# Eight weight parts queued at once in idle memory, at the head of a two-block transformer kernel

## The reference

```python
c_act = silu(c)                                   # [1, 1024]
for i in range(2):
    mod = c_act @ ada_w[i] + ada_b[i]             # ada_w[i]: 1024 x 6144
    sh_a, sc_a, g_a, sh_f, sc_f, g_f = split(mod, 6)
    h = rms_norm(x, norm_g[i, 0]) * (1 + sc_a) + sh_a
    y = attention_i(h, qkv weights, output weights, rel_bias)
    x = x + g_a * rms_norm(y, norm_g[i, 1])
    h = rms_norm(x, norm_g[i, 2]) * (1 + sc_f) + sh_f
    x = x + g_f * rms_norm(swiglu(h), norm_g[i, 3])
# then the third block, whose weights stream in the same way
```

## Time and profile before

| what | value |
|---|---|
| median of 3 runs | 1074.29 us (1073.21 to 1080.11) |
| span of the profiled execution | 1076.4 us |
| PE busy | 994.9 us (92%) |
| DVE busy | 690.4 us (64%) |
| ACT busy | 507.4 us (47%) |
| DMA, mean rate over the span | 193 GB/s |
| DMA, mean rate in the first 80 us | 337 GB/s |

### The profile page before, as it was taken

How to read it: one execution, slowest core, us unless ns; L and a number is a source line. 1 busy time by engine, 2 the same in 40 slices (tenths; PEclk the granted TensorE clock), 3 DMA queues, 4 the chain that set the end, 5 groups by cost and what they waited for, 6 DMA issues and landing times.

```text
span 1076.4 us, 18734 instructions
## 1 busy us (share of the span) xinstructions
PE 994.9 (92%) x7732; PEld 956.7 (89%) x7732; DVE 690.4 (64%) x724; ACT 507.4 (47%) x609; POOL 51.3 (5%) x103
## 2 busy tenths in 40 slices
PE   1799997999999997999889999999899999999996
PEld 1699995999999986999869999999799899999996
DVE  4787865778668747688755444444697654554554
ACT  2455435444344355566654343344565544444464
POOL 3010001001000001000010000000100000000000
PEclk9999989999999998999989999999999999999998
DMA  9997862598779741754215554556135465556511
GB/s 334 354 317 273 313 217 91 196 312 276 257 272 325 256 139 57 237 183 149 91 67 169 183 195 163 188 193 205 61 132 182 124 190 193 164 188 194 171 65 40
DMA packets 128186, 207.67 MB, mean 193 GB/s; under 512 B 4498, under 2 KB 101907, under 8 KB 128147
## 3 DMA queue, kind: packets, MB, share of 16 engines
q1 hardware_dynamic: 116818, 163.59, 45.9%
q0 software_dynamic: 11328, 43.53, 11.7%
HBM read 206.04 MB, written 1.06 MB: 192 GB/s over the span
## 4 chain that ended last, share of the span: by engine, by line
PE 83%; DVE 6%; ACT 4%; issue 3%; DMA 3%; POOL 1%; SPq 0%; DVEq 0%; POOLq 0%; ACTq 0%
PE ps L501 25%; PE ps L502 25%; PE ps L503 25%; PE ps L563 4%; DMA raw<-in_moba_w_qkv 2%; DVE rstd L1208 1%; ACT w_hi L857 1%; DMA ada_raw<-in_ada_w 1%; PE ps L678 1%; PE ps L576 1%; PE ps L652 1%; POOL xt L474 1%; DVE ada_sum L1177 1%; DVE w_lo L1164 1%; DVE y L1227 1%
## 5 line engine op out<-in xcount | busy, mean ns | idle before, releaser
L1164 DVE TENSOR_TENSOR w_lo<-raw,w_hi 128x2048 fp32r<-128x2048 f32 x145 | 332.0, 2291 | 220.2 <-ACT w_hi L857 220.0
L501 PE MATMUL ps<-h_hi,w_hi 128*128 128x256 f32 x1376 | 397.3, 289 | 23.0 <-DVE h_lo L1222 12.8
L857 ACT ACTIVATE w_hi<-raw 128x2048 fp32r<-128x2048 f32 x145 | 276.7, 1910 | 267.4 <-PE ps L503 265.9
L502 PE MATMUL ps<-h_lo,w_hi 128*128 128x256 f32 x1376 | 392.7, 285 | 0.0
L503 PE MATMUL ps<-h_hi,w_lo 128*128 128x256 f32 x1376 | 392.4, 285 | 0.0
L501 PEld LDWEIGHTS ps<-h_hi,w_hi 128*128 128x128 f32 x1376 | 267.6, 194 | 27.4 <-issue 23.3
L502 PEld LDWEIGHTS ps<-h_lo,w_hi 128*128 128x128 f32 x1376 | 267.9, 195 | 0.3
L503 PEld LDWEIGHTS ps<-h_hi,w_lo 128*128 128x128 f32 x1376 | 267.5, 194 | 0.0
L501 PE MATMUL ps<-o_hi,w_hi 128*128 128x256 f32 x528 | 155.1, 294 | 5.5 <-DVE o_lo L1482 2.3
L502 PE MATMUL ps<-o_lo,w_hi 128*128 128x256 f32 x528 | 150.0, 284 | 0.0
L503 PE MATMUL ps<-o_hi,w_lo 128*128 128x256 f32 x528 | 149.9, 284 | 0.0
(11 more groups left out here) (227 smaller groups left out, 1063.2 us busy)
## 6 DMA issues: line engine op xcount, KB each, us to landing
raw<-in_ffn_w_in SPq DMA_DIRECT2D x44, 1024.0 KB, 5.2
ada_raw<-in_ada_w POOLq DMA_DIRECT2D x40, 1024.0 KB, 5.8
raw<-in_ffn_w_out SPq DMA_DIRECT2D x22, 1024.0 KB, 5.0
raw<-in_w_up SPq DMA_DIRECT2D x16, 1024.0 KB, 5.5
raw<-in_w_down SPq DMA_DIRECT2D x16, 1024.0 KB, 4.9
raw<-in_moba_w_qkv SPq DMA_DIRECT2D x12, 1024.0 KB, 7.3
raw<-in_diff_w_qkv SPq DMA_DIRECT2D x12, 1024.0 KB, 5.5
raw<-in_w_in SPq DMA_DIRECT2D x6, 1024.0 KB, 5.4
```

The costliest lines, as they stand in the source:

```text
L501: T.matmul(out_ap, hi_s, hi_m, start=start, stop=False, skip_group_check=True)
L502: T.matmul(out_ap, hi_s, lo_m, start=False, stop=False, skip_group_check=True)
L857: A.activation(w_hi[:, n.place], raw[:, n.place], ACT.Copy).then_inc(slab_hi, 1)
L1164: V.tensor_tensor(w_lo[:, n.place], raw[:, n.place], w_hi[:, n.place].bitcast(F32), ALU.subtract).then_inc(slab_lo, 1)
```

## The change

Each of the first eight parts has a place that nothing else uses at that time: part 0 the tile `bias`, part 1 one half in `qkv` and one in `prob`, parts 2, 3 and 4 the places 2, 1 and 0 of `raw`, parts 5, 6 and 7 the places 0, 1 and 2 of `ada_raw`. SP issues all eight with no wait between them, `x` still behind part 1. Because a place may now be in two tiles, each part is issued as two transfers of 512 KB in place of one of 1 MB. The fourteen small vectors are issued behind part 7; before, they stood between part 5 and part 6. Slab 0 waits for `ada_acc` 10, slab 1 for 8, slab 2 for 6. The two loads of `bias` wait for `ada_acc` 2. The computation is the same.

```diff
         def first_mod_place(m):
-            if 3 <= m < 6:
-                return raw[:, m - 3].rearrange("p (k n) -> p k n", k=2), first_mods[m % 6]
-            return ada_raw[:, (m + 1) % ADA_RING], first_mods[m % 6]
+            if m == 0:
+                return bias_flat[:, 0:D], bias_flat[:, D:2 * D]
+            if m == 1:
+                return flat_qkv[:, 0:D], flat_prob[:, 0:D]
+            if m < 5:
+                return raw[:, 4 - m, 0:D], raw[:, 4 - m, D:2 * D]
+            place = (m + 1) % ADA_RING
+            return ada_raw[:, place, 0], ada_raw[:, place, 1]
...
                 else:
-                    sp.wait_ge(ada_acc, 2 * (n.first + 4))
+                    sp.wait_ge(ada_acc, 2 * (5 - n.first))
...
             def first_mod(m):
-                buffer, done = first_mod_place(m)
-                if m >= 6:
-                    sp.wait_ge(ada_acc, 2 * (m - 5))
-                sp.dma_start(buffer, rows(ada_w[0][:, ds(m // 4 * D, D)], m % 4)).then_inc(done, 16)
+                part = rows(ada_w[0][:, ds(m // 4 * D, D)], m % 4)
+                for k, buffer in enumerate(first_mod_place(m)):
+                    sp.dma_start(buffer, part[:, k]).then_inc(first_mods[m], 16)

             first_mod(0)
             first_mod(1)
             sp.dma_start(x_tok, ...).then_inc(x_loaded, 16)
-            for m in range(2, 6):
+            for m in range(2, 8):
                 first_mod(m)
...
             for dst, r, n, src in vectors:
                 sp.dma_start(dst[r:r + n, :], src).then_inc(rows_loaded, 16)
-            first_mod(6)
-            first_mod(7)
...
             for first, at, width in ((0, 0, S), (P, S, P)):
+                pool.wait_ge(ada_acc, 2)
                 src = bass.AP(line_dram.tensor, first, [[1, P], [LINE, HEADS], [1, width]])
                 pool.dma_start(bias[:, :, at:at + width], src).then_inc(bias_loaded, 16)
```

More of the change, by code:

```diff
@@ L226, in build @@
         bias_flat = bias[:].rearrange("p a b -> p (a b)")
+        flat_qkv = qkv[:].rearrange("p a b c -> p (a b c)")
+        flat_prob = prob[:].rearrange("p a b -> p (a b)")
         lru_h = bias_flat[:, 0:CT * S].rearrange("p (t s) -> p t s", t=CT)
@@ L247, in build @@
         slab_hi, slab_lo, slab_done = sem("slab_hi"), sem("slab_lo"), sem("slab_done")
-        first_mods = [sem(f"first_mods_{i}") for i in range(6)]
+        first_mods = [sem(f"first_mods_{i}") for i in range(8)]
         ada_loaded = [sem(f"ada_loaded_{i}") for i in range(ADA_RING)]
@@ L1165, in split_lo, with ada @@
                                 ALU.subtract).then_inc(slab_lo, 1)
-            def ada(m, place, count, slot, scalars, fresh, buffer=None, loaded=None):
-                buffer = ada_raw[:, place] if buffer is None else buffer
-                dve.wait_ge(loaded or ada_loaded[place], count)
+            def ada(m, place, count, slot, scalars, fresh, first_halves=None):
+                halves = first_halves or (ada_raw[:, place, 0], ada_raw[:, place, 1])
+                if first_halves:
+                    dve.wait_ge(first_mods[m], 32)
+                else:
+                    dve.wait_ge(ada_loaded[place], count)
                 for k in range(2):
                     if fresh and k == 0:
-                        V.tensor_scalar(ada_sum[:, slot], buffer[:, k], scalars[k], None, ALU.mult)\
+                        V.tensor_scalar(ada_sum[:, slot], halves[k], scalars[k], None, ALU.mult)\
                             .then_inc(ada_acc, 1)
@@ L1176, in ada @@
                         dve.wait_ge(ada_acc, m * 2 + k)
-                        V.scalar_tensor_tensor(out=ada_sum[:, slot], in0=buffer[:, k], scalar=scalars[k],
+                        V.scalar_tensor_tensor(out=ada_sum[:, slot], in0=halves[k], scalar=scalars[k],
                                                in1=ada_sum[:, slot], op0=ALU.mult, op1=ALU.add)\
@@ L1186, in ada_static @@
                 if m < 8:
-                    buffer, loaded = first_mod_place(m)
-                    ada(m, place, 32 if m >= 6 else 16, slot, c_cols(m % 4), m % 4 == 0, buffer, loaded)
+                    ada(m, place, 0, slot, c_cols(m % 4), m % 4 == 0, first_mod_place(m))
                 else:
```

## The result

The changed kernel takes 1082.07 us (median of 20 runs, 1077.77 to 1084.82) against 1077.84 us before (20 runs, 1073.21 to 1080.30). The ratio is 1.0042, 95% interval 1.0029 to 1.0054: 4.5 us slower (3.1 to 5.8); the two medians lie 4.2 us apart. The three runs of before that the prediction had gave 1074.29 us; twenty give 3.55 us more. The profiled execution of the changed kernel took 1079.86 us, with a span of 1078.2 us.

A forecast was written before the change was run, and what follows sets the result against it. PE bounds the kernel after a head set by full DMA engines and SP's in-order queue. Vectors landing later add 4.4 us at the first matmul, all other terms 0: 1074.29 + 4.4 = 1078.7 us, range 1073.9 to 1082.0.

The forecast's parts named there:

- The range: Whole kernel: the measured time was to lie between 1073.9 and 1082.0 us.
- about 1.5 us either way from the spread of the medians: Whole kernel: allowance added to the forecast's 3.7 to 5.0 us, giving 1076.5 to 1081 us.
- The vectors move behind parts 6 and 7: SP's queue in the head: vectors land at 35.1 us, not 30.04; PE starts 5.0 us later (4.3 to 5.6).
- What is behind PE's wait: Sums, root, reductions, flips after the vectors: same order, root at 42.1 us, first matmul at 48.4 us, 4.4 us later.
- Halves, 0: SP and DMA in the head: eight more transfers cost 0 to 0.5 us, taken as 0.
- Slab 0's later gate and the earlier issue of parts 6 and 7, 0: SP's queue: slab 0 issued at 25.6 us still lands at 37.6; issuing parts 6 and 7 earlier brings nothing; both 0.
- The bias waits: POOL's bias loads: `ada_acc` 2 is reached at 9.98 us, loads issue at 13.56 us; 3.6 us of cover, so 0.
- part 8, which waits for part 5 anyway: POOL's queue behind the bias loads: part 8 is held by its wait for part 5, so no cost, 0.
- TensorE's clock has no part: PE in the head: granted clock was 1.00, the 2.4 GHz level, even while idle, so no effect.
- the vectors are not held up: Rival, chance 0.13, SP's queue: PE starts near 30 us as before; time 1073.7 to 1074.3 us.
- A gain has a ceiling of 0.6 us: End of the head: even with slab 0 earlier, the root at 37.05 us bounds any gain to 0.6 us.

The follow-up runs named there:

- e2: Kernel before with only the fourteen small vectors issued behind part 7; ratio 1.0038 to the kernel before.
- e4: Changed kernel with every part but part 1 issued as one 1 MB transfer again; ratio 1.0042 to the kernel before.
- e8: Changed kernel with vectors back between parts 5 and 6, and POOL holding parts 8 and up until ACT has rounded slab 0; ratio 0.9991 to the kernel before.
- e7: Kernel before with only the two POOL waits for `ada_acc` 2 added ahead of the bias loads; ratio 1.0029 to the kernel before.
- e3: Changed kernel with the vectors issued right behind `x`, ahead of part 2; ratio 1.0024 to the kernel before.
- e6: Changed kernel with the vectors issued from ACT's own queue behind `c_act`, not SP's; ratio 1.0023 to the kernel before.
- e10: Kernel before with bias loads waiting until ACT has rounded slab 0 and the first three turned banks behind slab 0's matmuls; ratio 0.9950 to the kernel before.
- e5: Changed kernel with vectors behind `x`, bias loads waiting for slab 0's rounding, first three turned banks behind slab 0's matmuls; ratio 0.9952 to the kernel before.

## Why the prediction was right, and where not

- **Direction, mechanism and size of the difference** were right: 4.4 us were forecast, 4.5 measured (3.1 to 5.8), 4.62 us at the first matmul.
- **The range** missed by 0.07 us (1082.07 against 1082.0). The step that failed is "about 1.5 us either way from the spread of the medians". The median that it was added to, of three runs, lay 3.55 us under that of twenty. Those three runs spanned 6.9 us, which was to be seen. The term was too small in any case: of all triples of the twenty runs only 45% have a median within 1.5 us of 1077.84. That it was this far off is bad luck: 1.6% of the triples have a median of 1074.29 us or less. 1074.29 x 1.0042 would have been 1078.8 us, against a forecast of 1078.7.
- **The vectors move behind parts 6 and 7** was right: 35.53 us measured, 35.1 forecast, 35.34 in e2. Part 7 landed at 33.8 us, not 33.5.
- **What is behind PE's wait** was right step by step: the root at 42.38 (42.1 forecast), the turned banks until 48.02 (47.9), first matmul at 48.66 (48.4).
- **Halves, 0**: right, by e4. The fit that the prediction quotes against them stands in the Trainium skill ("DMA: Bandwidth & Descriptors", Anatomy of one DMA) for transfers issued by GpSimd, and these are SP's; no run here tests it on its own ground.
- **Slab 0's later gate and the earlier issue of parts 6 and 7, 0**: right, by e8. Slab 0 was issued at 26.34 us (25.6 forecast) and landed at 37.7 (37.6).
- **"The bias waits"**: its own wait cost nothing, as stated. But the sentence behind it, "part 8, which waits for part 5 anyway", failed. The trace of before had the row that speaks against it: part 8 was issued 5.8 us after part 5 was used. Two more instructions on POOL end that, and by e7 this is worth 3.1 us. In the changed kernel it is covered by the vectors: slab 0 was all but through when POOL's bytes began behind 36 us, and kept 4.5 us to spare; in e4, the same head but for the halves, it landed at 39.1 us with 3.3 us to spare. So the sum came out right, though one of its zeros was right only under cover of another term.
- **"TensorE's clock has no part"** was right for the sum, but not by its reason, that the granted clock is 1.00 even while PE is idle: in the changed kernel it was 0.50 from 20 to 40 us, and the steps at 0.50 took no longer than at 1.00 in the kernel before (last section).
- **The rival "the vectors are not held up"** was false for the changed kernel, as e2 shows. Its price was wrong as well: it gave 1073.7 to 1074.3 us, no change or less. e3 and e6, whose vectors are early, are some 2.5 us slower than before.
- **"A gain has a ceiling of 0.6 us"** holds for this change. The head as such could give more, by e10, through bytes taken out of it and not through places.

## What to carry to other kernels

While the DMA engines are full, as in this head, issuing a transfer earlier moves nothing forward; only the order in the queue and the bytes ahead of the first thing needed do. Put the smallest transfers that anything waits for first or on another queue (here that took some 2 us off the changed kernel; e5, which does it, gains no more than e10, which does not), and push what is needed late (here 1.5 MB of biases) behind the first slab by a wait on the work that needs the bandwidth. A transfer that keeps out of the way only because its engine happens to be late is not protected: hold it by a wait, or an unrelated edit will let it go.

## What the runs showed that was not expected

Two waits that are met when POOL comes to them changed the time by 3.1 us (e7, 1.0029), by moving a load 5.3 us forward. And the load, once it moves, takes four fifths of the bytes from the slab beside it, by its larger packets.

The granted clock fell to 0.50, the 1.2 GHz level, while PE was idle in the changed kernel, where in the kernel before it had stayed at 1.00. Windows of the changed kernel, columns as in the earlier trace rows:

```profile
25.00:30.00 5.00, 0.00 (x0) 0.00 (x0) 2.73 (x3) 0.00 (x0) 0.00 (x0) 0.50 1.01 387
```

It is no effect of the longer wait: e7, whose PE is idle from 16.8 to 30.7 us, about as long as before, has 0.50 in the same window, and e2, whose PE is idle until 35.34 us, has 1.00. What sets it is open: there is one profile of each kernel, and none shows how much it differs between executions. It also cost nothing that shows: from the vectors' transpose to the end of the root there are 6.85 us in the changed kernel (35.53 to 42.38), partly at 0.50, against 7.01 us in the kernel before and 6.41 in e2, both at 1.00.
